# Attention scores in fours at the end of a softmax step, in a two-block transformer in fp32

## The reference, cut to what matters

```python
# family A: 6 heads of 64, dilated windows;  family B: 4 heads, two maps of 32 each;  family C: 6 heads, 64 + 32 rotary
def probs(q, k):                                        # family B
    s = jnp.einsum('bqhd,bkhd->bhqk', sl(q), k) * scale + bias
    return jax.nn.softmax(jnp.where(causal, s, -jnp.inf), axis=-1)
a = probs(q1, k1) - lam * probs(q2, k2)
return jnp.einsum('bhqk,bkhd->bqhd', a, v)
...
s = jnp.einsum('bqhd,bkhd->bhqk', qs, k) * scale        # family C: causal, q and k of 96
p = jax.nn.softmax(jnp.where(causal, s, -jnp.inf), axis=-1)
return jnp.einsum('bhqk,bkhd->bqhd', p, v)
...
h = layer_norm(DEEPNORM_ALPHA * x + heads @ w_o, ln1_g, ln1_b)
```

## Time and profile before

| | |
|---|---|
| Time, median of 3 runs | 2969.93 us (2968.88 to 2970.45) |
| Profiled execution, span | 2967.5 us (the 2.4 us to the median lie around the span) |
| TensorE busy | 2928.1 us, 99% of the span |
| VectorE, ScalarE, GpSimd busy | 1931.7, 1290.9, 262.3 us |
| TensorE in the chain that ended last | 90% |
| Attention, families B, A, C, first layer | 53.6 to 243.6 us of the span |

### The profile page before, as it was taken

The page is one execution under the profiler, slowest core; times in us unless marked ns, Lnnn a source line. Parts: engine busy times, 40 slices in busy tenths (PEclk is TensorE's granted clock), DMA queues, the critical chain, the costliest instruction groups (busy, mean ns, idle before and its releaser), DMA issues.

```text
span 2967.5 us, 39610 instructions
## 1 busy us (share of the span) xinstructions
PE 2928.1 (99%) x16618; PEld 2489.5 (84%) x16618; DVE 1931.7 (65%) x2835; ACT 1290.9 (44%) x2001; POOL 262.3 (9%) x207
## 2 busy tenths in 40 slices
PE   8999999999999999999999999999999999999998
PEld 6766899977667899978999998888888888889997
DVE  4576676764667577776556456667777794576676
ACT  4554444444535354453333244433333335254444
POOL 0232000011331000020000001010101021000000
PEclk9999999999999999999999999999999999999999
DMA  5114433332115432221121213121212133322232
GB/s 186 50 47 167 170 139 118 107 107 73 49 59 199 148 122 93 100 79 61 68 72 66 70 65 108 56 101 49 89 49 101 46 121 123 120 82 102 100 107 79
DMA packets 45074, 285.39 MB, mean 96 GB/s; under 512 B 5135, under 2 KB 5663, under 8 KB 19424
## 3 DMA queue, kind: packets, MB, share of 16 engines
q1 hardware_dynamic: 42480, 269.77, 25.7%
q0 software_dynamic: 2416, 13.09, 1.2%
HBM read 277.04 MB, written 5.79 MB: 95 GB/s over the span
## 4 chain that ended last, share of the span: by engine, by line
PE 90%; DVE 5%; ACT 4%; issue 1%; POOL 1%; DMA 0%; DVEq 0%; SPq 0%; POOLq 0%; ACTq 0%
PE ps L857 18%; PE ps L859 18%; PE ps L858 18%; PE ps L1117 9%; PE ps L1119 9%; PE ps L1118 9%; PE ps L1035 2%; PE ps L1048 1%; PE ps L1062 1%; DVE wlo L2021 1%; PE ps L956 1%; ACT whi L1381 1%; ACT SQL L1423 1%; PE ps L940 1%; ACT A1h L1442 0%
## 5 line engine op out<-in xcount | busy, mean ns | idle before, releaser
L2021 DVE TENSOR_TENSOR wlo<-wraw,whi 128x1536 fp32r<-128x1536 f32 (+2 forms) x221 | 425.3, 1924 | 238.3 <-ACT whi L1381 238.3
L1381 ACT ACTIVATE whi<-wraw 128x1536 fp32r<-128x1536 f32 (+2 forms) x221 | 353.3, 1599 | 458.3 <-PE ps L859 385.9
L857 PE MATMUL ps<-A1h,whi 128*128 128x512 f32 x1024 | 412.0, 402 | 8.4 <-DVE A1l L2042 7.6
L859 PE MATMUL ps<-A1h,wlo 128*128 128x512 f32 x1024 | 400.4, 391 | 0.0
L858 PE MATMUL ps<-A1l,whi 128*128 128x512 f32 x1024 | 399.9, 391 | 0.0
L1117 PE MATMUL ps<-A1h,whi 128*128 128x256 f32 (+1 forms) x836 | 245.6, 294 | 2.4 <-DVE wlo L2021 1.6
L1119 PE MATMUL ps<-A1h,wlo 128*128 128x256 f32 (+1 forms) x836 | 244.4, 292 | 0.0
L1118 PE MATMUL ps<-A1l,whi 128*128 128x256 f32 (+1 forms) x836 | 244.3, 292 | 0.0
L857 PEld LDWEIGHTS ps<-A1h,whi 128*128 128x128 f32 x1024 | 193.6, 189 | 52.1 <-issue 11.8
L859 PEld LDWEIGHTS ps<-A1h,wlo 128*128 128x128 f32 x1024 | 192.8, 188 | 41.2
L858 PEld LDWEIGHTS ps<-A1l,whi 128*128 128x128 f32 x1024 | 193.3, 189 | 39.0 <-issue 2.2
(11 more groups left out here) (528 smaller groups left out, 7196.6 us busy)
## 6 DMA issues: line engine op xcount, KB each, us to landing
wraw<-wstream SPq DMA_DIRECT2D x159, 1024.0 KB, 4.9
MW<-wstream SPq DMA_DIRECT2D x34, 1024.0 KB, 6.9
wraw<-wstream SPq DMA_DIRECT2D x42, 768.0 KB, 4.3
wraw<-wstream SPq DMA_DIRECT2D x34, 640.0 KB, 3.9
wraw<-wstream SPq DMA_DIRECT2D x4, 960.0 KB, 4.7
hk<-gd POOLq DMA_DIRECT2D x1, 2560.0 KB, 13.4
X<-xT SPq DMA_DIRECT2D x4, 512.0 KB, 6.9
sx<-X POOLq DMA_DIRECT2D x1, 2048.0 KB, 7.6
```

The lines of the kernel that those rows point to most:

```text
L857: mm(o, l[0], r[0], start=start, stop=False)
L859: return mm(o, l[1], r[0], start=False, stop=stop)
L1381: act(whi[i_ % 2][:, 0:n], wraw[i_ % 2][:, 0:n], ACT.Copy, bias=0.0, scale=1.0).then_inc(ev("hi", i_).by(act_whi), 1)
L2021: tt(wlo[i_ % 2][:, 0:n], wraw[i_ % 2][:, 0:n], raw(whi[i_ % 2][:, 0:n]), SUB).then_inc(ev("lo", i_).by(dve_wlo), 1)
```

## The change

The scores of four sets are issued in one piece, at the end of a step in place of its start. In B that is every second step, with both maps of both heads of a pair for one block. In A and C it is every fourth step, with both heads of a pair for two blocks. In C the first halves of all four come before the four rotary halves. The other engines have no share in the piece `scores`, and the order of their pieces stays. The four sets hold four of the seven banks. In `WO_TILES` the first group of three output tiles becomes one of two and one of one.

```diff
-WO_TILES = ((0, ((0, 1, 2),)), (3, ((0,), (1,), (2,))), (6, ((0,), (1,))))
+WO_TILES = ((0, ((0, 1), (2,))), (3, ((0,), (1,), (2,))), (6, ((0,), (1,))))
...
-        if step < n and (here == "B" or step % 2 == 0):
-            put("scores", *items[step])
         if 0 <= step - 1 < n:
             put("exps", *items[step - 1])
...
         while due >= 1.0:
             due -= 1.0
             next(filler, None)
+        if step < n and step % (2 if here == "B" else 4) == 0:
+            put("scores", *items[step])
...
                         kd, h, i = x
-                        n = 128 * (i + 1)
+                        four = [(h_, i, m) for h_ in (h, h + 1) for m in range(2)] if kd == "B" else [(h_, i_, 0) for i_ in (i, i + 1) for h_ in (h, h + 1)]
...
-                        for h_, m in ((h, 0), (h, 1)) if kd == "B" else ((h, 0), (h + 1, 0)):
-                            b = AB.hold("s", l, kd, h_, i, m)
+                        for h_, i_, m in four:
+                            b, n = AB.hold("s", l, kd, h_, i_, m), 128 * (i_ + 1)
                             q, k = qk_of(kd, h_, m)
                             e.wait_ge(b.before)
-                            last = mm(b.ap[:, 0:n], q[:, 128 * i:128 * i + 128], k[:, 0:n], start=True, stop=kd != "C")
+                            last = mm(b.ap[:, 0:n], q[:, 128 * i_:128 * i_ + 128], k[:, 0:n], start=True, stop=kd != "C")
                             if kd != "C":
                                 last.then_inc(b.full.by(product), 1)
                         if kd == "C":
-                            for h_ in (h, h + 1):
-                                b = AB.of("s", l, kd, h_, i, 0)
+                            for h_, i_, _ in four:
+                                b, n = AB.of("s", l, kd, h_, i_, 0), 128 * (i_ + 1)
                                 q, k = qk_of(kd, h_, 1)
-                                mm(b.ap[:, 0:n], q[:, 128 * i:128 * i + 128], k[:, 0:n], start=False, stop=True).then_inc(b.full.by(product), 1)
+                                mm(b.ap[:, 0:n], q[:, 128 * i_:128 * i_ + 128], k[:, 0:n], start=False, stop=True).then_inc(b.full.by(product), 1)
```

## The result

The changed kernel is slower. Median 2986.49 us (2984.76 to 2988.04, 4 runs) against 2969.4 us of the kernel before on the same chip (2968.79 to 2970.45, 4 runs): ratio 1.0057, 95% interval 1.0045 to 1.0069. Nine runs of it in two series have the median 2984.8. The forecast was 2974, with a range to 2981: the sign of the sum was right, the size was not.

What follows compares the result with a forecast made beforehand. TensorE, busy 99% of the 2967.5 us span, was taken as the bound. Waits of 12.0 less savings of 6.6 and 3.3 gave 2.1 us a layer, 4.3 for two: span 2971.8, time 2974 us, range 2962 to 2981.

Steps and rivals of the forecast that it cites:

- Part 4: Output tile grouping (`WO_TILES`) and the SP and POOL queues, which keep their order: claimed to change nothing.
- Part 3: Scores at the end of a step, in B, A and C: new TensorE waits of 12.0 us a layer.
- W3: End of B, filler used up: `turn` of (B, 2, 2) waits for late `probs`, 2.0 us.
- W4: A: a four ahead of the sum `latent q` delays the chain to `pv`; wait 1.9, 1.7 more than before.
- W1: Step 4 of B: fourth matmul of scores (B, 0/1, 2) waits for the bank of (B, 1, 1), 1.7 us.
- W2: B, next after W1: a `vA mm` waits for the bank of (B, 2, 2), map 0, 0.6 us.
- W5: A, around `turn` (A, 3, 0): VectorE's unbroken row and the bank of (A, 3, 3) add 1.3 us of wait.
- W6: End of A, no filler for eight steps: `min` of (A, 4, 2) waits for `pv` and a four, 3.0 us more.
- Parts 1 and 2: Scores savings a layer: B's four maps side by side 6.6 us, merged query blocks in A and C 3.3 us.
- rival 3: B's fours run two by two, so 5.0 us a layer of savings are lost: 2981 us, chance 0.13.
- Rival 2: A's waits W4 to W6 are absent, 6.0 us a layer less: 2962 us, chance 0.2.
- Rival 4: More waits on other banks, each missed one 1 to 2 us a layer: 2980 us, chance 0.17.

## Why the prediction was wrong

Two terms that it put at nothing failed, and a third was mis-sized. Either of the two alone would have left the time at the upper edge of the range, 2981: the kernel with filled waits has 2981.1 (median of ten), that without GpSimd's work 2980.4.

**The clock, which stands in the first paragraph: "Clock 1.00 throughout, DMA share under 0.2: neither enters."** This step took the clock of the kernel before as given, and the new waits then made TensorE idle. The granted clock fell to 1.2 GHz behind some of them, each fall cost 1.5 us, and the two traces of the changed kernel have six and three of them. Filling the waits gives back some 4 us of the median (2984.8 against 2981.1). In the execution that was profiled the clock cost 8.7: its span is 18.5 us longer, it reached the attention 0.8 earlier, and 2 x 5.3 of the 19.3 are there without a fall. The Trainium skill (TensorE: Matmul & The Clock Gate, Part 1: The HAM clock gate) says that an idle TensorE is gated down to half its clock, and, of the turn to full clock at a kernel's start, that its place differs between runs of one kernel. The traces agree with the first at 1.2 GHz (0.50 in the rows), and are in keeping with the second, in that equal waits of 2.65 us had a fall behind them once and once not.

**Part 4, the queue of GpSimd at nothing, and durations in Part 3 taken over as they stood.** GpSimd's splits keep their order, but the pieces beside them moved. In the kernel before the stretched instructions of VectorE lie where nothing waits (cutting GpSimd's work gains nothing there), after the change two of them lie in the chains to W3 and W4. Worth 2.4 us a layer by the medians (2980.54 - 2975.75, over two), 2.5 in the second layer of the traces with filled waits: 0.7 up to the second `pv` of B, 1.0 from there to A's first, 0.1 to A's last, 0.8 to C's last. In the median that is as much as the clock. The Trainium skill (GPSIMD Engine Reference, 8. Key points) says that GpSimd shares its SBUF interfaces with VectorE, whose instructions with two SBUF inputs or in a 2-port mode collide with it; the rows agree, a product of two 128x1 inputs that takes 0.16 us took 0.86.

**Part 3, the waits.** A wait costs 0.17 us more than its idle time, since a matmul's record lasts 0.39 us and the next could have come after 0.22. With that (an estimate), a layer of the changed trace has, beyond the kernel before:

| | forecast | measured |
|---|---|---|
| W1, bank of (B, 1, 1) | 1.7 | 1.8 |
| W2, bank of (B, 2, 2) | 0.6 | 0.5 |
| W3, turn (B, 2, 2) | 2.0 | 2.8; 2.1 without GpSimd |
| W4, first `pv` of A | 1.7 | 2.3; 1.3 without GpSimd |
| W5 | 1.3 | 1.0 |
| W6, end of A | 3.0 | 3.0 |
| C | 1.7 | 3.2 |
| elsewhere | 0 | 0.5 to 0.9 |

The sum is 15 to 15.5 in place of 12.0. The mechanism (the first `min` of a four waits for it, and what is queued behind) and nearly all places were right; C was mis-sized by half, and fours in C alone, even by the forecast, cost 2.2 us a layer. Of the signs, the turn of (B, 2, 2) comes 4.15 us after its four (forecast 3.3), and 3.45 without GpSimd's work. A's first `pv` comes 9.33 after `cq`'s last matmul in place of 7.24, so 2.1 later where the forecast had 0.9; the four, which now stands between that matmul and the turn, is 0.9 of it, and GpSimd 1.0.

**Parts 1 and 2, the savings.** The fours of B run four wide, as taken; the bound of two by two is excluded by the eight records in 1.07 us, and rival 3 with it. With 15 to 15.5 us of waits and 5.3 net, some 10 was saved a layer (worked out, not measured by itself), the forecast's 9.9.

**Rivals.** Rival 2 (no waits in A) is out by the trace. Rival 4 (more waits, on banks) comes near with its 2980, but not by its cause: of the 13.5 us of waits in the first layer 3.8 are on ScalarE's exp. No rival had the clock or GpSimd. Without both the kernel stands at 2975.8, beside the forecast of 2974: the walk was good in sum (too little in C, a little too much in W4 and W5), and what it left out cost 9 us in the median. `WO_TILES` was nothing, as said.

What stays open: C's waits were not taken apart one by one, and what decides whether the clock falls behind a given wait.

## What to carry to other kernels

Price each new wait of the engine that bounds twice: by its length, and, where it idles TensorE, by a fall of the clock that may come behind it, here 1.5 us each and not in every run (behind waits of 0.87 to 2.65 us). When pieces are moved, lay the queues of VectorE and GpSimd side by side at the new places: a row's duration holds for the neighbours that it had. A merge that saves on the bounding engine is, here, best made only where its results are not awaited and banks are free: six of the twenty fours of a layer gave 6 us in all, all twenty cost 14 to 17. And a number that comes out right is no proof of the theory behind it: look in the trace whether its parts are there.

## What the runs showed of the hardware

- Four fp32 matmuls of 32 rows on four partition groups take hardly longer than two: 1.07 us against 1.06 for 512 keys, 0.65 against 0.63 for 256.
- TensorE's clock fell to 1.2 GHz for some 3.4 us at a time (6.8 once, with fours in A alone), behind idle stretches of 2.65 and 2.45 us, behind two of 0.91 and 1.19 us close together, behind one of 1.76 us at 1371 us, where the kernel before had 1.75 and no fall, and, with fours in B alone, behind one of 0.87 us. The same wait with the same length had a fall in one layer and none in the next.
- In such a stretch fp32r matmuls follow each other at 0.43 us in place of 0.23.
- With matmuls that are thrown away put into the waits, the clock stayed up in attention, and a layer cost 5.1 to 5.2 us, no more than the 5.3 of one without them and without a fall.
- A VectorE instruction from SBUF to SBUF took up to 1.3 us in place of 0.27, and one with two inputs of 128x1 0.86 in place of 0.16, while GpSimd was in an instruction of its own; those on PSUM (`min`, 0.70 us) did not.
